# A fifth weight place, whole-matrix transfers and a residual put in by TensorE in a hybrid attention and mixture-of-experts block

## The reference

```
h2 = rmsnorm(x, ffn_norm_g)
logits = h2 @ router_w + router_b;  top 4 of 32 -> softmax -> comb[token, expert]
for e in range(32):
    g = min(h2 @ w_gate[e] + b_gate[e], 7)
    u = clip(h2 @ w_up[e] + b_up[e], -7, 7)
    act = (u + 1) * g * sigmoid(1.702 * g)
    out += comb[:, e] * (act @ w_down[e] + b_down[e])
x + out
```

## Time and profile before

| | us |
|---|---|
| median of 3 runs | 1101.21 (1101.12 to 1103.13) |
| the profiled execution | 1100.92 |
| its span | 1099.1 |
| TensorE busy | 1058.1 (96%) |
| VectorE busy | 276.5 (25%) |
| ScalarE busy | 188.8 (17%) |
| GpSimd busy | 30.2 (3%) |

### The profile page before, as it was taken

The page is one execution under the profiler, slowest core; times in us unless marked ns, Lnnn a source line. Parts: engine busy times, 40 slices in busy tenths (PEclk is TensorE's granted clock), DMA queues, the critical chain, the costliest instruction groups (busy, mean ns, idle before and its releaser), DMA issues.

```text
span 1099.1 us, 12598 instructions
## 1 busy us (share of the span) xinstructions
PE 1058.1 (96%) x5124; PEld 449.3 (41%) x5124; DVE 276.5 (25%) x564; ACT 188.8 (17%) x340; POOL 30.2 (3%) x43
## 2 busy tenths in 40 slices
PE   9999999999999999999999999999999999999997
PEld 5889984333333333333333333333333333333332
DVE  6876563111111111111111111111111111111112
ACT  4656622000100010001000100010000100010000
POOL 0070020000000000000000000000000000000000
PEclk9999999999999999999999999999999999999999
DMA  9734697999999999999999999999999999999996
GB/s 315 292 112 161 231 394 298 419 428 427 427 429 429 429 429 428 429 429 428 428 428 428 428 429 429 429 429 428 429 429 427 428 429 428 428 429 429 429 428 253
DMA packets 43966, 432.95 MB, mean 394 GB/s; under 512 B 6021, under 2 KB 6570, under 8 KB 19370
## 3 DMA queue, kind: packets, MB, share of 16 engines
q1 hardware_dynamic: 43472, 432.38, 94.1%
q10 hardware_dynamic: 474, 0.30, 0.1%
HBM read 431.61 MB, written 1.05 MB: 394 GB/s over the span
## 4 chain that ended last, share of the span: by engine, by line
PE 50%; DMA 39%; DVE 7%; ACT 2%; issue 1%; SPq 0%; DVEq 0%; ACTq 0%
PE ps L831 35%; DMA ring<-in_exp_w_up 19%; DMA ring<-in_exp_w_gate 19%; PE ps L803 3%; PE ps L532 2%; PE ps L534 2%; PE ps L533 2%; PE ps L796 2%; PE ps L837 2%; DVE arena L1425 2%; DVE ring_r L1151 2%; DMA ring<-in_w_in 1%; DVE arena L1423 1%; ACT ring_r L892 1%; PE ps L855 0%
## 5 line engine op out<-in xcount | busy, mean ns | idle before, releaser
L831 PE MATMUL ps<-ring,arena 128*64 128x512 f32 x3072 | 688.3, 596 | 23.9 <-DMA ring<-in_exp_w_gate 20.2
L831 PEld LDWEIGHTS ps<-ring,arena 128*64 128x64 f32 x3072 | 210.6, 137 | 440.9 <-issue 384.0
L1413 DVE TENSOR_SCALAR arena<-ps 128x512 f32<-128x512 f32 x32 | 22.1, 691 | 475.5 <-PE ps L831 475.5
L1423 DVE TENSOR_SCALAR arena<-ps 128x512 f32<-128x512 f32 x32 | 22.1, 692 | 235.0 <-PE ps L831 235.0
L1046 ACT COPY arena<-ps 128x512 f32<-128x512 f32 x32 | 18.8, 586 | 318.9 <-PE ps L790 318.9
L803 PE MATMUL ps<-arena 64*128 64x512 f32 x264 | 65.6, 615 | 0.8 <-ACT arena L1052 0.8
L1044 ACT ACTIVATE arena<-arena 128x512 f32<-128x512 f32 x32 | 20.1, 629 | 258.6 <-DVE arena L1413 258.6
L790 PE MATMUL ps<-arena 128*64 128x512 f32 x264 | 62.3, 592 | 0.7 <-DVE arena L1360 0.7
L532 PE MATMUL ps<-ring_r 128*128 128x256 f32 (+1 forms) x192 | 59.3, 309 | 0.7 <-DVE arena_r L1239 0.3
L1052 ACT COPY arena<-ps 128x512 f32<-128x512 f32 x32 | 18.7, 586 | 235.0 <-PE ps L831 235.0
L533 PE MATMUL ps<-ring_r 128*128 128x256 f32 (+1 forms) x192 | 57.7, 300 | 0.0
(11 more groups left out here) (200 smaller groups left out, 589.0 us busy)
## 6 DMA issues: line engine op xcount, KB each, us to landing
ring<-in_exp_w_gate SPq DMA_DIRECT2D x64, 2048.0 KB, 32.8
ring<-in_exp_w_up SPq DMA_DIRECT2D x64, 2048.0 KB, 35.3
ring<-in_exp_w_down SPq DMA_DIRECT2D x64, 2048.0 KB, 34.4
ring<-in_w_in SPq DMA_DIRECT2D x7, 2048.0 KB, 9.3
ring<-in_w_out SPq DMA_DIRECT2D x2, 2048.0 KB, 8.0
xt<-in_x SPq DMA_DIRECT2D x4, 512.0 KB, 7.5
ring<-in_w_in SPq DMA_DIRECT2D x4, 512.0 KB, 8.3
ring<-in_pool_up SPq DMA_DIRECT2D x1, 2048.0 KB, 7.7
```

The costliest lines, as they stand in the source:

```text
L831: last = mm(ps[BLOCK * half:BLOCK * (half + 1), bank, :], src[:, c, k % 2, :], slot(n)[:, c, HALF * half:HALF * (half + 1)], start=False, ...
L1413: v.tensor_scalar(g1, ps[:, 4, :], LIMIT, None, ALU.min).then_inc(g_ready, 1)
L1423: v.tensor_scalar(u1, ps[:, 5, :], LIMIT, -LIMIT, ALU.min, ALU.max).then_inc(expert_step, 1)
```

## The change

- The tiles of attention that are dead once its output is transposed, 32 KB a partition, form one region (`hold_front`); with the ring's eight slots taken in pairs there are five places of 32 KB, one matrix each (`HOLDS`). The other small tiles are laid out anew over each other; some buffers that were double are single.
- The weights are loaded by matrix (`load_matrix`). Gate and up come in one transfer of 4 MB, 32 KB a partition; down comes in two halves with a semaphore each. The first matrix is issued from inside the front's list of pieces, after the biases and ahead of w_out's second half, and waits for the transposes of attention's output; the next four wait for the ring. From the sixth on, a matrix waits for both products of the matrix five before it, and a down's first half for the first of them.
- The last expert's up and down have their second half in two transfers of 1 MB each.
- The residual is put into the four output sums by multiplies with the identity (`start_from_residual`) in place of the clearing and of some `keep_clock` fillers; after the last scatter ScalarE and VectorE copy two sums each, and ScalarE sends one of them out itself.
- The loop holds ten experts and runs three times; the last two experts stand behind it. Only the last has `final` set: it gathers nothing for a next expert. The first round stands by itself, further rounds behind an `If`.
- ScalarE makes the normalised rows of the first half of the tokens (VectorE did), and the assignment of weight rows to partitions follows the new transfers.

The diff, cut to its core:

```diff
-UNROLL = 4
+UNROLL = 10
 STEPS = E // UNROLL
 PIECES_PER_EXPERT = 6
-ARENA = 16400
+MATRICES = 3
+HOLDS = 5
+HOLD = 2 * PIECE
+ARENA = HOLD + 10896
...
+        hold_front = part(HOLD)
+        taken[0] = 0
         vtok = part(NT * 512).rearrange("p (t c) -> p t c", t=NT)
...
-        LEFT_BY = [GB1, GB1, AUP_P, AUP_P, WO_P, WO_P, WO1, WO1]
+        LEFT_BY = [None, GB1, AUP_P, WO_P, WO1]
...
+        def hold(k):
+            if k == 0:
+                return hold_front.rearrange("p (h x) -> p h x", h=2)
+            return ring[:, 2 * (k - 1):2 * k, :]
+
+        def hold_chunks(k):
+            return hold(k).rearrange("p h (c n) -> p h c n", c=4)
+
+        def landings(k):
+            return MATRICES * E // HOLDS + (1 if k < MATRICES * E % HOLDS else 0)
+
+        def lowers(k):
+            return len([n for n in range(2, MATRICES * (E - 1), MATRICES) if n % HOLDS == k])
...
+        TAIL_PARTS = ((0, 2), (2, 4))
...
+            def load_matrix(r, base, n):
+
+                k, m = n % HOLDS, n % MATRICES
+                of_round = r * (E * PIECES_PER_EXPERT) + base * PIECES_PER_EXPERT
+                at_start = isinstance(base, int) and n < HOLDS
+                if not at_start:
+                    first_half, both_halves = 2 * (n - HOLDS) + 1, 2 * (n - HOLDS) + 2
+                    sp.wait_ge(piece_done, of_round + (first_half if m == 2 else both_halves))
+                elif not isinstance(r, int):
+                    sp.wait_ge(piece_done, r * (E * PIECES_PER_EXPERT))
+                elif n == 0:
+                    sp.wait_ge(o_T, NT)
+                else:
+                    front_piece_free(sp, LEFT_BY[n])
+                expert = base + n // MATRICES
+                last = n // MATRICES == E - 1
+                name = ("exp_w_gate", "exp_w_up", "exp_w_down")[m]
+                if m == 0 or m == 1 and not last:
+                    src = A[name][0].rearrange("e (p r) n -> p e (r n)", p=P)[:, bass.ds(expert, 1), :]
+                    sp.dma_start(hold(k).rearrange("p h x -> p (h x)"),
+                                 src.rearrange("p e x -> p (e x)")).then_inc(matrix_in[k], 16)
+                    return
+                by_half = "e (p h c) n -> p e h c n" if m == 1 else "e (h p c) n -> p e h c n"
+                src = A[name][0].rearrange(by_half, p=P, h=2)[:, bass.ds(expert, 1)].rearrange("p e h c n -> p h (e c n)")
+                sp.dma_start(hold(k)[:, 0, :], src[:, 0, :]).then_inc(matrix_in[k], 16)
+                if m == 2 and not at_start:
+                    sp.wait_ge(piece_done, of_round + both_halves)
+                if not last:
+                    sp.dma_start(hold(k)[:, 1, :], src[:, 1, :]).then_inc(lower_in[k], 16)
+                    return
+                for i, cols_i in enumerate(TAIL_PARTS):
+                    part_i = slice(D * cols_i[0], D * cols_i[1])
+                    sp.dma_start(hold(k)[:, 1, part_i], src[:, 1, part_i]).then_inc((tail_up, tail_down)[m - 1][i], 16)
+
+            def load_round(r):
+                for n in range(HOLDS, MATRICES * UNROLL):
+                    load_matrix(r, 0, n)
+                with sp.Fori(1, STEPS) as step:
+                    for n in range(MATRICES * UNROLL):
+                        load_matrix(r, step * UNROLL, n)
+                for n in range(MATRICES * UNROLL * STEPS, MATRICES * E):
+                    load_matrix(r, 0, n)
...
@@ -477,42 +543,31 @@
                             half = row // 2
                             sp.dma_start(bias_raw[E * row:E * (row + 1), k, :],
                                          A[name][0][:, HALF * half:HALF * (half + 1)]).then_inc(bias_in, 16)
+                    load_matrix(0, 0, 0)
                 if n == GB_P + 1:
 
                     sp.wait_ge(qk_T, 4)
...
+            for n in range(1, HOLDS):
+                load_matrix(0, 0, n)
+            load_round(0)
...
+            for i, (t, half) in enumerate(((0, 0), (0, 1), (1, 1))):
+                part_cols = slice(HALF * half, HALF * (half + 1))
+                if half == 0:
+                    sp.wait_ge(act_out_ready, t + 1)
+                else:
+                    sp.wait_ge(dve_out_ready, t + 1)
+                sp.dma_start(out[0, P * t:P * (t + 1), part_cols], y_out[:, t, part_cols]).then_inc(out_done, 16)
...
             def keep_clock(n, bank):
+                pe.wait_ge(bias_ready, 1)
                 for _ in range(n):
-                    mm(ps[:, bank, :], m_split[1][:, 2, 0:P], m_split[1][:, 0:2, :].rearrange("p c s -> p (c s)"),
-                       start=True, stop=True)
+                    mm(ps[:, bank, :], bias_rows[:, 0, 0:P], bias_rows[:, 1, :], start=True, stop=True)
+
+            def start_from_residual(t, half):
+                mm(ps[:, 2 * t + half, :], ident, xt[:, t, HALF * half:HALF * (half + 1)], start=True, stop=True)
...
-            keep_clock(3, 4)
-
-            for b in range(4):
-                mm(ps[:, b, :], zrow[:, 0:P], zrow[:], start=True, stop=True)
+            start_from_residual(0, 0)
+            start_from_residual(0, 1)
...
-            keep_clock(3, 4)
+            start_from_residual(1, 0)
+            keep_clock(1, 4)
...
+                def product(k, bank, src):
+                    n = MATRICES * j + k // 2
+                    at = n % HOLDS
+                    parts = tail_up if k == 3 else tail_down
+                    if k == 5 and not final:
+                        pe.wait_ge(lower_in[at], r * (16 * lowers(at)) + step * (16 * MATRICES * UNROLL // 15) + 16 * (n // 15 + 1))
+                    elif k % 2 == 0:
+                        pe.wait_ge(matrix_in[at], r * (16 * landings(at)) + step * (16 * MATRICES * UNROLL // HOLDS)
+                                   + 16 * (n // HOLDS + 1))
+                    for c in range(4):
+                        if final and k in (3, 5):
+                            for i, cols_i in enumerate(TAIL_PARTS):
+                                if c == cols_i[0]:
+                                    pe.wait_ge(parts[i], r * 16 + 16)
+                        for half in range(2):
+                            last = mm(ps[BLOCK * half:BLOCK * (half + 1), bank, :], src[:, c, k % 2, :],
+                                      hold_chunks(at)[:, k % 2, c, HALF * half:HALF * (half + 1)],
+                                      start=False, stop=(k % 2 == 1 and c == 3), skip_group_check=True)
+                    last.then_inc(piece_done, 1)
...
+                if final:
+                    turn_weights(6)
+                    pe.wait_ge(act_ready, done + (j + 1))
+                    turn(7, act_out).then_inc(act_T, 1)
+                else:
+                    pe.wait_ge(pick_ready, done + (j + 2))
+                    gather(1 - buf)
+                    pe.wait_ge(act_ready, done + (j + 1))
+                    turn(7, act_out).then_inc(act_T, 1)
+                    turn_weights(5)
+                    pe.wait_ge(hg_ready, done + (j + 2))
+                    turn(6, h_got).then_inc(h_turned, 1)
...
-            keep_clock(2, 4)
+            start_from_residual(1, 1)
...
+            experts(0)
+            with pe.If(rounds > 1):
+                with pe.Fori(1, rounds) as r:
+                    pe.wait_ge(pick_ready, r * E + 1)
+                    gather(0)
+                    pe.wait_ge(hg_ready, r * E + 1)
+                    turn(6, h_got).then_inc(h_turned, 1)
+                    experts(r)
...
-            nc.scalar.copy(bias_rows, bias_raw).then_inc(bias_hi, 1)
+            nc.scalar.copy(bias_first, bias_raw).then_inc(bias_hi, 1)
...
+            def normed(t):
+                for half in range(2):
+                    fn(h2[:, t, HALF * half:HALF * (half + 1)].rearrange("q (c p) -> q p c", c=4),
+                       xt[:, t, :].rearrange("q (p h c) -> q p h c", h=2, c=4)[:, :, half, :], ACT.Copy,
+                       scale=rstd[:, t:t + 1]).then_inc(h2_ready, 1)
...
+            act.wait_ge(wo_done, wo_count(1, 1))
+            act.wait_ge(x2_root, 1)
+            normed(0)
...
+            for t in range(NT):
+                act.wait_ge(scattered, 2 * t + 1)
+                nc.scalar.copy(y_out[:, t, 0:HALF], ps[:, 2 * t, :]).then_inc(act_out_ready, 1)
+            act.wait_ge(act_out_ready, NT)
+            act.dma_start(out[0, P:S, 0:HALF], y_out[:, 1, 0:HALF]).then_inc(out_done, 16)
...
+            for t in range(NT):
+                dve.wait_ge(scattered, 2 * t + 2)
+                v.tensor_copy(y_out[:, t, HALF:D], ps[:, 2 * t + 1, :]).then_inc(dve_out_ready, 1)
```

More of the change, by code:

```diff
@@ new lines, in build @@
+        left, expo, logit, combf, ranks = [act_flat[:, NT * E * i:NT * E * (i + 1)].rearrange("p (t e) -> p t e", t=NT)
+                                           for i in range(5)]
+        act_out = act_flat
+        assert taken[0] == places["gate"]
+        h2 = part(NT * D).rearrange("p (t d) -> p t d", t=NT)
```

(63 more changed lines are left out.)

313 lines of the change are left out of this document (129 added, 184 removed).

## The result

| | before | after |
|---|---|---|
| median (5 runs each) | 1101.82 (1101.12 to 1103.13) | 1107.55 (1107.23 to 1108.95) |
| profiled execution, its span | 1100.92, 1099.1 | 1107.57, 1105.8 |
| first product of expert 0 | 178.64 | 185.25 |
| last expert's gate landed, TensorE goes on | 1067.83 | 1069.90 |
| from there to the end of the span | 31.27 | 35.90 |

The ratio is 1.0053, interval 1.0038 to 1.0068: slower, where I forecast 1098.2 and at most 1103.5. I write "the landing" for the fourth row. Until then I had forecast -5.6 us (terms 1, 2, 3 and 7) and got +2.1; behind it +2.6 (terms 4 to 6) and got +4.6.

What follows compares the result with a forecast made beforehand. Weight transfers were taken as the bound, unbroken at about 428 GB/s once restarted; -9.8 + 3.9 + 4.0 + 0.1 + 2.9 - 0.9 + 0.6 - 3.8 = -3.0 us gave 1098.2 us as median, range 1094 to 1103.5.

Steps and rivals of the forecast that it cites:

- terms 1: Expert weight ring: a fifth place loaded before the restart gives -9.8 us, coarser release +3.9, net -5.9.
- Term 2: Front, w_out's projection: its second half lands late behind the first expert matrix, delaying the restart, +4.0 us.
- term 3: Rest of the front: identity multiplies replacing fillers, moved normalisation and single buffers cost +0.1 us.
- term 7: Gate and up transfers: 32 KB rows instead of 16 KB save a fixed cost per row, -3.8 us, bounds 0 and 5.
- Term 4: Last expert: gate arrives whole under one semaphore, so its products wait for all of it, +2.9 us.
- Term 5: Output: two copies each on ScalarE and VectorE replace four additions in a row on VectorE, -0.9 us.
- term 6: Code layout: skipped branch before the last scatter, +0.6 us; the loop's jump shows no fetch wait, body perhaps held.
- Rival B: w_out's delay mostly hidden, GpSimd keeping 0.80 us beside VectorE: restart moves 1.8 instead of 4.0, 1096.0 us; 15%.
- rival C: Front loses more than the place brings as the granted clock falls: restart moves by 9.5, 1103.7 us; 13%.
- A: Rival on the weight flow: the rate stays 428 GB/s despite longer rows, 1102.0 us, no change; 25%.

Runs made afterwards that it cites:

- e2: The changed kernel with five experts in the loop instead of ten and three small buffers in turn: 1101.75 us, ratio 0.9997.
- e3: The kernel before the change with sixteen experts in the loop instead of four, nothing else: 1108.32 us, ratio 1.0052.
- e10: The changed kernel with the first round's 32 experts written out in a row, no jump back: 1106.2 us, ratio 1.0028.
- e12: e8 with the first round's 32 experts written out instead of a loop of five: 1096.81 us, ratio 0.9942.
- e1: The changed kernel with the first expert matrix issued behind w_out's second half instead of ahead of it: 1098.24 us, ratio 0.9964.
- e11: The changed kernel with VectorE's low parts of w_out's second half after GpSimd's, four small operations moved behind the first residual: 1100.25 us, ratio 0.9983.
- e4: The changed kernel with the last expert's gate in two halves, each with its own semaphore: 1105.8 us, ratio 1.0036.
- e8: e6 with the last expert's gate in two halves, each with its own semaphore: 1091.55 us, ratio 0.9911.
- e5: e8 with eight idle multiplies added in the last expert, where the gather is missing: 1091.15 us, ratio 0.9905.
- e7: e6 with gate and up in two transfers of 16 KB rows, TensorE waiting for both: 1099.16 us, ratio 0.9977.
- e6: The changed kernel with w_out's second half ahead of the first expert matrix and five experts in the loop: 1093.94 us, ratio 0.9927.
- e9: e6 with the fifth matrix loaded behind the first product, so four matrices are in at the restart: 1099.39 us, ratio 0.9965.

## Why the prediction was wrong

**The step that failed: term 6 and its last sentence.** I priced the longer code only as one skipped branch at the end (0.6 us) and passed over the loop ("shows nothing of it, as its body may still be held"). That sentence held the answer: with four experts the body is held and 13 fetches serve the whole run, with ten it is not, and 47 are made. The branch costs nothing that shows (0.78 us before the scatter in both, time that ScalarE's copy takes anyway). The fetches cost 5.8 us by e2 (6.1 by rows) and 6.0 by e3 (5.4 by rows); 4.2 to 4.7 us come without any jump (e10, e12), and at most 1.9 with the jumps. They move 0.48 MB more than in e2, which would be 1.1 us at 430 GB/s if all 16 DMA engines shared it evenly. It costs five times that, because a fetch takes its engine for 1.57 us and about half of the engines carry all of them: a weight matrix is complete only with its slowest engine. Why a fetch takes 1.0 to 1.1 us where a weight packet of the same 16 KB takes 0.61 stays open.

The Trainium skill (Runtime: NRT & Kernel Launch, Instruction fetch mechanics) has the wait at a taken branch, and calls the streaming of further code mostly hidden. The first is small here and the second does not hold where the flow of transfers is the bound: e10 and e12 have only the streaming.

**Term 2, w_out late: +4.0 forecast, 7.5 measured (e1).** Landing, casts and GpSimd's start were right to 0.3 us. The size of one subtraction was wrong: I took 1.22 us from a single record, but that one began after a wait, and eight back to back, most of them beside VectorE, take 1.39 on average. Bank and restart moved 2.5 us further than term 2 and 3 allow (6.6 against 4.1). e11 shows the contention by taking it away. Rival B had the wrong sign, and rival C the right sign with the wrong mechanism: the granted clock did fall in the changed kernel (0.58 from 144 to 146, 0.50 from 146 to 150), but e2 is granted 1.00 there and its first product starts within 0.1 us of it. GpSimd sets the pace there and hides the clock. It hides it only while GpSimd is still at work (until 154.4): in e4 and e10 the clock is 0.50 up to 156, and their first products come at 186.61 and 187.32, 1.4 and 2.1 us later than in the changed kernel (in e10 GpSimd also starts 0.5 us later). So rival C's mechanism exists, at this size, in some executions. Rival B's own working was also 0.2 off: at 0.80 us each the bank ends at 150.1, which is +1.6 and not +1.8.

The Trainium skill (SBUF — State Buffer, Who interferes with whom) gives the two engines one shared pair of ports under an exclusive lock. The runs nearly agree: in the 6.23 us of VectorE's four, 4.63 are its own time alone, and GpSimd, at one start each 1.67 us there, has 6.23 / 1.67 x 0.70 = 2.6 of its own; together 7.2, so about one us was shared.

**Term 4, gate whole: +2.9 forecast, +3.0 in the profile** (16.5 behind the landing against 13.5). The split returned 1.6 of it, in e4 and in e8.

**Not forecast: +1.6 us at the end.** The last expert has no gather; TensorE waits 1.49 and 0.68 us in a row, the granted clock is 0.50 from 1090 to 1092, and the last down pair takes 8.65. In other kernels of this family, the same pair takes 7.04 (e4, e5, e7, e8, e10, e11) or 8.2 to 9.9 (e1, e2, e6, e9, e12), each time with a stretch at 0.50 in it. e8 has the same two waits (1.49 and 0.68) without one. What decides between them I can't say.

**Term 5, output: -0.9 forecast, 0 measured.** The last copy does end sooner behind the scatter, but four transfers now go out almost together: 2.4 and 2.9 us to land where it was 2.2.

**Held: terms 1 and 7, and term 3 within a microsecond.** The fifth place is worth 5.7 where I said 5.9 us net (e9), the rest of the front is 0.9 faster where I said 0.1 slower (by e1), and the longer rows give 4.6 to 5.2 where I said 3.8 (e7), so A falls.

The sum in rows: the forecast -3.0, +2.5 for the restart (terms 2 and 3), +6.1 for the fetches, +1.6 for the clock, +0.9 for the output, -0.6 for the branch and +0.1 for the gate make +7.6, against +6.7 measured. The 0.9 left over is of the size that the longer rows give beyond term 7 by rows (4.6 against 3.8); that they are the same is not shown.

## What to carry to other kernels

Where transfers bound a loop, the size of its body is a cost of its own: read the instruction row among the DMA queues, and compare it between loop lengths, before a longer unrolling is counted as free. Price it by the DMA engine that carries most of it, not by its share of all 16. A transfer issued ahead of one that the critical path needs costs the whole of its bytes, and then whatever the late work collides with. Take a contended duration from a run of records that stand back to back, not from one.

## What the runs showed of the hardware beyond that

- Bodies of four and five experts (13 and 18 fetches) run without repeated fetches; ten and sixteen (47 and 43) don't. The limit lies between five and ten experts here. Written out without a loop, the same code makes 42 (e10, e12).
- GpSimd and VectorE slow each other on float32 subtractions: 0.70 us alone against 1.39 for 128x256, and 1.16 against 1.56 for 128x1024.
- A fetch of 16 KB holds up its DMA engine by 1.57 us in the middle of a flow of weights, and about half of the 16 engines carry all fetches.
- 32 KB rows in one transfer, against 16 KB rows in two, give 4.6 us over the run by rows and 5.2 by medians, where the line through 2, 4 and 16 KB rows says 3.8.
